# Rotary partner rows by transfers in the first block, and the gate chain moved ahead of the queries in the second

## What is computed

```python
def _rope(x, cos, sin):
    x1, x2 = jnp.split(xf, 2, axis=-1)
    out = jnp.concatenate([x1 * c - x2 * s, x2 * c + x1 * s], axis=-1)
...
    q = _rope(q.reshape(bsz, seq, N_DIFF_HEADS, 2, DIFF_HEAD_DIM), cos, sin)
    k = _rope(k.reshape(bsz, seq, N_DIFF_HEADS, 2, DIFF_HEAD_DIM), cos, sin)
    o = _diff_attention(q, k, val, lam_full)
```

```python
def log_decay(z_lr, w_alpha, b_alpha):
    z = jnp.einsum('bldr,drk->bldk', z_lr.reshape(B, L, 2, GLA_GATE_RANK), w_alpha) + b_alpha
    la = jnp.maximum(jax.nn.log_sigmoid(z.astype(jnp.float32)) / GLA_GATE_TAU, GLA_LOG_ALPHA_MIN)
...
    b = jnp.cumsum(log_a, axis=2)      # within chunks of 64
    q_dec = qc * jnp.exp(b)
    k_inv = kc * jnp.exp(-b)
```

## Time and profile before

| | us |
|---|---|
| median of 3 runs | 1823.71 |
| lowest, highest | 1823.33, 1826.53 |
| the profiled execution, its own time | 1826.43 |
| its span in the trace | 1824.7 |

### The profile page before, as it was taken

The page is one execution under the profiler, slowest core; times in us unless marked ns, Lnnn a source line. Parts: engine busy times, 40 slices in busy tenths (PEclk is TensorE's granted clock), DMA queues, the critical chain, the costliest instruction groups (busy, mean ns, idle before and its releaser), DMA issues.

```text
span 1824.7 us, 31051 instructions
## 1 busy us (share of the span) xinstructions
PE 1789.1 (98%) x12824; PEld 1618.3 (89%) x12824; DVE 1136.3 (62%) x1735; ACT 866.2 (47%) x1412; POOL 249.4 (14%) x264
## 2 busy tenths in 40 slices
PE   9999999999999999999999999999999899999998
PEld 8998699999899879997899997999787777889998
DVE  5764686686666466656675776566645555655553
ACT  5453344664445435443435753545345345445443
POOL 2000232121200020002321212000111343100000
PEclk9999999999999999999999999999999999999999
DMA  8565654446566666755745455675553333355553
GB/s 289 188 229 191 227 185 162 162 139 198 195 205 211 208 205 227 238 186 173 260 150 182 140 185 196 222 234 184 172 171 91 95 90 107 116 172 181 188 188 105
DMA packets 252397, 330.58 MB, mean 181 GB/s; under 512 B 13162, under 2 KB 213072, under 8 KB 252256
## 3 DMA queue, kind: packets, MB, share of 16 engines
q1 hardware_dynamic: 248240, 315.31, 53.0%
q0 software_dynamic: 4016, 13.27, 2.1%
HBM read 327.51 MB, written 1.05 MB: 180 GB/s over the span
## 4 chain that ended last, share of the span: by engine, by line
PE 62%; issue 24%; DVE 6%; POOL 3%; ACT 2%; DMA 2%; SPq 0%; POOLq 0%; DVEq 0%; ACTq 0%
PE bank L716 14%; PE bank L719 14%; PE bank L717 14%; PE bank L739 4%; PE bank L741 4%; PE bank L742 4%; DVE X L1939 1%; DMA G<-in_lam_dram 1%; DVE wlo L1861 1%; PE bank L1278 1%; ACT whi L1408 1%; POOL rs L2459 1%; PE bank L1256 1%; PE bank L904 1%; PE bank L942 1%
## 5 line engine op out<-in xcount | busy, mean ns | idle before, releaser
L1861 DVE TENSOR_TENSOR wlo<-raw,whi 128x1024 fp32r<-128x1024 f32 x537 | 664.2, 1241 | 383.6 <-ACT whi L1408 379.7
L1408 ACT ACTIVATE whi<-raw 128x1024 fp32r<-128x1024 f32 x549 | 574.2, 1051 | 390.5 <-PE bank L742 166.1
L716 PE MATMUL bank<-XTh,whi 128*128 128x256 f32 x1984 | 559.9, 282 | 0.0
L719 PE MATMUL bank<-XTh,wlo 128*128 128x256 f32 x1984 | 551.1, 278 | 0.0
L717 PE MATMUL bank<-XTl,whi 128*128 128x256 f32 x1984 | 550.8, 278 | 0.0
L716 PEld LDWEIGHTS bank<-XTh,whi 128*128 128x128 f32 x1984 | 373.4, 188 | 2.9
L717 PEld LDWEIGHTS bank<-XTl,whi 128*128 128x128 f32 x1984 | 374.0, 189 | 1.0
L719 PEld LDWEIGHTS bank<-XTh,wlo 128*128 128x128 f32 x1984 | 372.8, 188 | 0.4 <-DVE wlo L1861 0.3
L716 PE MATMUL bank<-HCh,whi 128*128 128x256 f32 (+1 forms) x880 | 252.4, 287 | 0.6 <-DVE tmp L2355 0.6
L717 PE MATMUL bank<-HCl,whi 128*128 128x256 f32 (+1 forms) x880 | 248.3, 282 | 0.0
L719 PE MATMUL bank<-HCh,wlo 128*128 128x256 f32 (+1 forms) x880 | 248.2, 282 | 0.0
(11 more groups left out here) (344 smaller groups left out, 2425.7 us busy)
## 6 DMA issues: line engine op xcount, KB each, us to landing
raw<-in_ffn_w_dram SPq DMA_DIRECT2D x131, 1024.0 KB, 5.1
raw<-in_w_in_dram SPq DMA_DIRECT2D x76, 1024.0 KB, 5.0
raw<-in_w_mod_dram SPq DMA_DIRECT2D x24, 1024.0 KB, 5.1
raw<-in_w_branch_dram SPq DMA_DIRECT2D x16, 1024.0 KB, 4.9
raw<-in_w_out_dram SPq DMA_DIRECT2D x12, 1024.0 KB, 4.8
raw<-in_w_ffn_gate_dram SPq DMA_DIRECT2D x11, 1024.0 KB, 5.2
raw<-in_w_ffn_up_dram SPq DMA_DIRECT2D x11, 1024.0 KB, 5.1
raw<-in_w_ffn_down_dram SPq DMA_DIRECT2D x8, 1024.0 KB, 5.2
```

Of the source, the lines that this page charges most:

```text
L716: e.matmul(o, hi[:, k, w0:w0 + nc_], xh, start=first and k == 0, stop=False)
L719: m = e.matmul(o, lo[:, k, w0:w0 + nc_], xh, start=False, stop=last and k == nk - 1)
L1408: e.activation(hi_part(n), raw_part(n), ACTF.Copy).then_inc(WHI.did(n), 1)
L1861: e.tensor_tensor(lo_part(n), raw_part(n), hi_part(n).bitcast(F32), ALU.subtract).then_inc(WLO.did(n), 1)
```

## The change

In the first block the 32 permutation matmuls are gone. The straight rows `s` stay, and the swapped rows are written by four transfers of 32 partitions and 256 columns each into the tile `u`: two by SP, two by POOL. `mtmp` has eight tiles, the constant table loses the permutation matrix, and each of the eight new semaphores (`ROT`, `ROTP`) serves every fourth projection. DVE multiplies by cos one step and by sin two steps behind the projection. SP issues the transfers of projections 2m and 2m + 1 behind the load that it makes then. POOL issues its transfers of projection n ahead of the addition for n - 2, and its load of the norm's factors (`load_gb`) stands at n = 5. In the second block z is projected first, the gate products stand behind qg 0, ACT's `g1` and `g2` and DVE's `g1` and `g2` stand beside qg and q, ACT's `g3` ahead of k, and POOL's products with decays ahead of the additions for k. `settle` is added in `mod_columns` and once ahead of qk 0. The low halves of weights are unchanged.

```diff
@@ plan @@
     for k in (0, 4):
         chunk_b(w, k, 4, 2048, 512, MOVES)
+    chunk_a(w, 0, 8, 3072, 32)
     chunk_a(w, 0, 8, 1536)
     for k in (0, 4):
         chunk_b(w, k, 4, 0, 512, MOVES)
-    chunk_a(w, 0, 8, 3072, 32)
@@ program @@
-            mtmp = some(st, "mtmp", 4, [128, T])
+            mtmp = some(st, "mtmp", 8, [128, T])
...
-            r = Ring(4)
+            r = Ring(8)
             for n in range(16):
-                r.use(("s", n), (SMALL, ("perm", l, n)), (DMX, ("cos", l, n)))
-                if n:
-                    r.use(("u", n - 1), (PMX, ("rot", l, n - 1)))
+                r.use(("s", n), (ROT[n % 4], ("turned", l, n)), (ROTP[n % 4], ("turned", l, n)), (DMX, ("cos", l, n)))
+                r.use(("u", n), (PMX, ("rot", l, n)))
@@ sync @@
+            def turned(l, n):
+                ring_free(q, tm[l], ("u", n))
+                q.wait_ge(AMX, ("qk", l, n))
+                for p in (0, 32):
+                    e.dma_start(mtmp[tm[l].slot["u", n]][p:p + 32, :], mtmp[tm[l].slot["s", n]][p ^ 32:(p ^ 32) + 32, :]).then_inc(
+                        ROT[n % 4].did(("turned", l, n), by=16), 16)
...
             for c in range(1, before_bias):
                 load(c)
+                for l in range(2):
+                    if first_qk[l] <= c - 4 < first_qk[l] + 8:
+                        for j in range(2):
+                            turned(l, 2 * (c - 4 - first_qk[l]) + j)
@@ tensor: mod_columns, mixer @@
-                mm.then_inc(MOD.did(("columns", g)), 1)
+                settle(b).then_inc(MOD.did(("columns", g)), 1)
...
-                def rotate(n):
-                    b = 4 + n % 2
-                    q.wait_ge(AMX, ("qk", l, n))
-                    empty(b)
-                    e.matmul(bank[b][:, 0:T], perm, mtmp[tm[l].slot["s", n]][:, :], start=True, stop=True).then_inc(
-                        SMALL.did(("perm", l, n)), 1)
-                    emptied[b] = ((DMX, ("sin", l, n)),)
-
+                empty(3)
+                settle(3)
                 for n in range(16):
...
-                    if n:
-                        rotate(n - 1)
@@ tensor: second @@
+                b = B2["z"]
+                empty(b)
+                gemm_a(bank[b][0:32, :], xj, "z", nc_=32)
+                emptied[b] = ((A2, "z"),)
+                for n in range(2):
+                    b = B2["qg", n]
+                    empty(b)
+                    gemm_a(bank[b][:, 0:T], xx, ("qg", n))
+                    emptied[b] = ((A2, ("qg", n)),)
+                    if n == 0:
+                        g1()
...
                     headturn("turnq", n, NT[ntr.slot["q", n]])
-                    if n == 0:
-                        g1()
@@ vector: mixer @@
+                norm_v(0)
                 for n in range(16):
                     w.pass_by(1)
+                    if n == 0:
+                        norm_v(1)
                     if n:
-                        rotate(n - 1)
+                        times_cos(n - 1)
+                    if n > 1:
+                        times_sin(n - 2)
+                times_cos(15)
@@ vector: second @@
+                w.pass_by(2)
+                g1()
+                w.pass_by(1)
+                w.more(1)
+                slots = [0, 1, 2]
+
+                def between_q():
+                    n = slots.pop(0)
+                    if n < 2:
+                        rope("permq", n, QG[:, n, :], NT[ntr.slot["qg", n]], tmp[t2r.slot["uq", n]], B2["permq", n], 0.125)
+                    g2(n)
+                w.pass_b(4, 2, between_q)
+                w.more(3)
+                g2(3)
...
+                headnorms("q", [NT[ntr.slot["q", t]] for t in range(2)])
@@ gpsimd: mixer @@
+                def turned(n):
+                    ring_free(q, tm[l], ("u", n))
+                    q.wait_ge(AMX, ("qk", l, n))
+                    for p in (64, 96):
+                        e.dma_start(mtmp[tm[l].slot["u", n]][p:p + 32, :], mtmp[tm[l].slot["s", n]][p ^ 32:(p ^ 32) + 32, :]).then_inc(
+                            ROTP[n % 4].did(("turned", l, n), by=16), 16)
```

More of the change, by code:

```diff
@@ L278, in plan @@
     parts = [(c, j) for c in range(len(chunks)) for j in range(len(chunks[c][3]))]
-    return chunks, parts, whole, on_dve, before_bias
+    return chunks, parts, whole, on_dve, before_bias, first_qk
 MOVES, STANDS = 48, 0
@@ L317, in hold @@
         held.update(at[name] for name in names)
-    for n in range(2):
-        nb(("qg", n))
+    nb("z")
+    nb(("qg", 0))
+    for db in range(4):
+        nb(("gate", db))
+    nb(("qg", 1))
     hold([("q", t) for t in range(2)])
@@ L395, in program @@
         BIAS = [signal(f"s_bias{h}") for h in range(8)]
+        ROT = [signal(f"s_rotary{i}") for i in range(4)]
+        ROTP = [signal(f"s_rotary_pool{i}") for i in range(4)]
         MM, TURN, SMALL, MOD = [signal("s_pe_" + n) for n in ("gemm", "turn", "small", "mod")]
@@ L825, in mod_columns @@
                 for j in range(4):
-                    mm = e.matmul(bank[b][:, 2 * j:2 * j + 2], spare[0:m, j * 128:(j + 1) * 128], cmb[0:m, :], start=True, stop=True)
-                mm.then_inc(MOD.did(("columns", g)), 1)
+                    e.matmul(bank[b][:, 2 * j:2 * j + 2], spare[0:m, j * 128:(j + 1) * 128], cmb[0:m, :], start=True, stop=True)
+                settle(b).then_inc(MOD.did(("columns", g)), 1)
                 emptied[b] = ((DMD, g),)
@@ L1114, in g1 @@
                         emptied[b] = ((D2, ("min", db)),)
+                b = B2["z"]
[9 more added lines that the diff above has]
+                        g1()
+                slots = [lambda: perm_g("permq", ("qg", 0), 0, B2["permq", 0]),
+                         lambda: perm_g("permq", ("qg", 1), 1, B2["permq", 1]), lambda: None]
+                gemm_b(("q",), 4, 2, xb, (0, 1), [[B2["q", t]] for t in range(2)], 512, tail=2, between=lambda: slots.pop(0)())
+                for t in range(2):
+                    emptied[B2["q", t]] = ((D2, ("turnq", t)),)
                 def g4():
@@ L1951, in mixer, with norm_v @@
                 w.more(3)
-                for t in range(2):
-                    if t:
-                        w.more(1)
+                def norm_v(t):
                     for c in range(2):
@@ L2253, in g9 @@
                                             v[:, 4 * t + h:4 * t + h + 1], None, ALU.mult).then_inc(D2.did("ogn"), 1)
-                for n in range(2):
-                    w.pass_by(1)
-                    if n == 0:
-                        g1()
-                    else:
-                        w.more(1)
-                        g2()
+                w.pass_by(2)
                 calls_k = [0]
@@ L2562, in second @@
                     e.tensor_copy(KG[:, n, T:512], NT[ntr.slot["kg", n]][:, T:512]).then_inc(P2.did(("kc", n)), 1)
[L2563 to L2565 removed]
+                q.wait_ge(P2, ("rotq", 1))
+                q.wait_ge(P2, ("kc", 1))
                 for db in range(4):
@@ L2570, in second @@
                     e.tensor_tensor(LA[:, db, T:512], LA[:, db, T:512], KG[:, db % 2, T:512], ALU.mult).then_inc(P2.did(("kw", db)), 1)
+                for n in range(2):
+                    rotate("k", n, KG[:, n, 0:T])
                 w.pass_b(4, 2, tiles=4)
```

189 lines of the change are left out of this document (81 added, 108 removed).

## The result

| | us |
|---|---|
| kernel before, median of 20 runs | 1822.99 |
| changed kernel, median of 20 runs | 1831.11 |
| ratio, with its 95% interval | 1.0047 (1.0035 to 1.0058) |
| changed kernel, profiled execution: own time, span | 1828.74, 1827.0 |

The account below looks back on a forecast made before the run. PE, busy 98% of the span, was taken to bound the kernel. Permutations -13.4, transfers 0, settling transposes +1.2 and second block +2.5 gave -9.7 us: 1814.0 us against the median of 1823.71, range 1804 to 1822.

Parts of the forecast that it names:

- The permutations, -13.4: First block: removing the 32 permutation matmuls from PE's path gains 6.7 us a layer, 13.4 us in two layers.
- The new wait for the low half of qk 4: First block, start of the stage: PE waits 1.4 us there for DVE's low half, in place of the old wait.
- What hides the transfers: First block: the small transfers replacing the permutations are covered by the distance between projections; cost taken 0.
- the bound of 7: First block: upper bound on the transfers' cost, 7 us a layer, with 0 as the lower bound.
- the loop over three projections: POOL, first block: two issues, landing, sin product and addition fit 8.46 us if landing takes up to 5.2; 3.1 taken.
- a split is made 5.6 us ahead of its use: DVE, first block: it may be late by 3 to 5 us, but PE does not see it.
- ACT's copy now waits for the transfers of four projections before: First block: ACT's copy waits for transfers by then 11.3 us old; within the transfers' cost of 0.
- Rival 2: First block: transfers land late, over 5.2 us on POOL, DVE's splits become the bound; 7.0 us a layer, 1828 us; chance 0.10.
- The settling transposes, +1.2: Seven transposes added in `mod_columns` and two ahead of qk 0, 0.13 us each, lose 1.2 us; bounds 0 and 2.8.
- The second block, +2.5: Second block: new PE wait of 7.8 us for normalized q, plus 0.2, less the old wait of 5.5: 2.5 us lost.
- the remaining wait for `SO`: Second block, transposes of k: of PE's old 5.5 us wait, 0.2 is left.
- The sum: Whole kernel: permutations, settling transposes and second block together give -9.7 us, 1814.0 us forecast.

## Why the prediction was wrong

**The permutations, -13.4: right.** Without transfers the stage is 7.0 us shorter in each layer (6.7 forecast), 5.8 where it ran at the wider distance throughout. The new wait for the low half of qk 4 is 1.44 in the trace (1.4 forecast), and 1.03 in the second layer:

```profile
242.97 0.39 PE L731 MATMUL bank<-XTh,wlo 128*128 128x256 f32 x1 [1.44 <-DVE wlo L1855]
```

**What hides the transfers, "Cost taken: 0": this is the step that failed.** It cost 11.0 and 11.4 us a layer in the first trace (60.34 and 60.72 less the 49.33 of the kernel without transfers), beyond the bound of 7 that I gave; in the second trace it cost 9.9 and 13.9. Three things in it were wrong, and the runs weigh them.
- The landing on POOL was taken as 3.1, from the row of the nearest size. In the stage it was 4.8 at the median and 7.4 at most in the first layer, 8.3 in the second, and the loop over three projections holds 5.2. The nearest row was so in size but not in what ran beside it: 32 KB alone landed in 1.7. The far bound that the prediction named, 8.2, was reached.
- "a split is made 5.6 us ahead of its use ... so PE does not see it." Of the splits that is nearly true, as the kernel with two steps and sixteen tiles shows. But a backlog of DVE does not vanish, since a round took DVE 2.35 us of PE's 2.72 (268.90 to 271.25 from one product with sin to the next) and so gave back 0.4 in each round. What it still owed when the 16 projections were over stood ahead of its additions for the gating, for which PE waits. The prediction looked for the cover up to the last projection and not at the next place where PE needs DVE.
- "ACT's copy now waits for the transfers of four projections before, 11.3 us old." They were 11.3 old only if issued on time. SP's stand behind a load that waits for low halves of DVE, and DVE's low halves behind the product that waits for a transfer: each round of lateness is handed on.

**Rival 2 was what happened**, in its mechanism and its point of decision (landings over 5.2 on POOL, DVE late), with a chance of 0.10. Its price, 7.0 a layer, took PE as slowed round by round. By the traces the loss is 10 to 14 a layer, in a few long waits and in the slow clock behind them, which it left out.

The prediction named the shared-port rule of the Trainium skill, page "SBUF — State Buffer", section "SBUF: two separate sides", beside this rival. By that rule the descriptors of POOL's transfers cannot be written while DVE holds the shared port pair. The trace does not bear it out as the cause: POOL's issues did not grow beside DVE's work, they took 1.00 to 1.08 us a pair, where the earlier trace rows has 0.58 for one. The page's 3.1 us is for a `tensor_copy` of DVE, which does not run in this stage. The transfers of SP, which do not come from POOL, landed later than POOL's, 4.9 against 4.0 at the median of the program. But no run here separates what lengthened POOL's landings.

**The settling transposes, +1.2: about right.** They were not run alone. By the distances of PE's rows one costs 0.09 in `mod_columns` and 0.12 ahead of qk 0 (1331.80 - 1330.73 = 1.07 between neighbours in the changed kernel, 0.98 before), 0.9 for nine.

**The second block, +2.5: right in the traces.** The wait is 7.9 for the forecast 7.8, the remaining wait for `SO` 0.2 for 0.2. Without the slow stretch of one execution the block is 1.5 to 3.5 us longer. The slow clock behind the long wait was set equal to that behind the old one. In the first pair of traces it held for 4.6 us of work (1395.58 to about 1400.2) against 3, some 0.8 us more. But it varies between executions: from 3.3 to 4.8 us behind the new wait in nine traces, and 2.9, 5.8 and 5.9 behind the old one in the three that have it. One pair does not size it, and that the two cancel is not refuted. The 2.9 is also why the block took 92.83 in the first trace of before: it took 94.24 in the second and 94.25 in the kernel with the first block's part alone. Only the timed runs of this part alone say more (3 to 11 us), and that gap is not explained. With the norm of q earlier, the second block's part alone gained 9 us by the medians, 14 by the ratios and 8.7 by the block in the traces.

**The sum.** In the first trace: 4.0 + 4.4 + 0.9 + 5.2 = 14.5 us longer, and the span is longer by 2.3. Most of the rest stands in the distance of matmuls. In the kernel before, 39% of the stretches of 256-column matmuls ran at the wider distance, in this trace of the changed one 12%: of some 8600 such matmuls 27% at 0.0045 us, 10 us; some 2 us stay open. It may also be why runs of one kernel spread over 10 us, which the traces, one or two of a kernel, do not show. It stands in no term of the forecast, and it favoured the changed kernel in the profiled execution, by luck.

## What to carry to other kernels

Before a transfer takes the place of an engine's step, count the loop that it closes, at the landing time that such a transfer has beside the loads of that stage and not alone; if the loop holds less than the longest landing, use the result a step later instead. One step more (three for two, with the same tiles) was worth 0.8% here. Where an engine that feeds the critical one falls behind, ask not only for its next deadline but for the first place at which its queue must be empty. And when one step is moved ahead of another on a helper engine, place it by its user's arrival: with two of the four rounds of decays ahead of the norm the old wait stayed away and the new one was 1.0 us, with all four it was 7.9.

## What was not expected of the hardware

**Two distances of matmuls.** A stream of 256-column matmuls ran at one of two constant distances, with the granted clock at 1.00 in both. Copies of ACT behind the u projections of layer 1 (24 matmuls each), 2.82 apart in the earlier trace rows and 2.72 in the changed kernel:

```profile
296.25 0.38 ACT L1499 ACTIVATE mtmp<-bank 128x256 f32<-128x256 f32 x1 [1.39 <-PE bank L731]
298.96 0.39 ACT L1499 ACTIVATE mtmp<-bank 128x256 f32<-128x256 f32 x1 [1.08 <-PE bank L731]
```

In the traces a stretch kept its distance until PE waited or did something else, and at times had the other one after it: in 13 of 20 stages without permutations the projections qk 0 to 3 were 2.83 apart and, behind the wait at qk 4, 2.72. In the stages with permutations u ran at 2.83 in all eight stages traced. What decides is open.

**Landing.** 32 KB from SBUF to SBUF took 1.7 us where little else moved (issued at 240.43). Beside 1 MB loads, in the stages of the changed kernel, it took 4.8 and 5.0 at the median on POOL's and SP's queue in the first layer, and 8.3 and 7.6 at most in the second; in the kernel with four steps and the load of the factors at n = 5 POOL's longest took 9.4.

**POOL beside DVE.** One addition of 256 columns took 0.75 us alone, 1.4 to 1.6 in mid-stage, and 3.79 at 245.15, where DVE ran two splits and three products almost without a pause. POOL's instructions in these kernels name SBUF tiles alone, no PSUM bank, so what the opening says of POOL working on PSUM is shown by nothing here.
